# Output projections of a two-layer encoder: residual in token rows, norms per row tile inside the projection, activations as the stationary operand

## The reference, cut to what matters

```python
def rms_norm(x, g):
    y = xf * lax.rsqrt(jnp.mean(xf * xf, axis=-1, keepdims=True) + EPS)
    return (y * g.astype(jnp.float32)).astype(x.dtype)
...
    return jnp.concatenate([y_a, y_b], axis=-1) @ w_out      # layer 0: (1040, 2048) @ (2048, 1024)
...
    return (hh * jax.nn.silu(z)) @ w_out                     # layer 1: the same shapes
```

## Time and profile before

| | us |
|---|---|
| median of 3 runs (lowest, highest) | 3476.79 (3475.44, 3481.76) |
| span of the profiled execution | 3469.1 |
| what lies around that span, to the median | 7.7 |
| PE busy, share of the span | 2705.0, 78% |
| DVE busy | 1420.7, 41% |
| ACT busy | 912.4, 26% |
| POOL busy | 1079.5, 31% |
| mean granted clock of PE, share of full | 0.891 |

### The profile page before, as it was taken

How to read it: one execution, slowest core, us unless ns; L and a number is a source line. 1 busy time by engine, 2 the same in 40 slices (tenths; PEclk the granted TensorE clock), 3 DMA queues, 4 the chain that set the end, 5 groups by cost and what they waited for, 6 DMA issues and landing times. The chain is left out here.

```text
span 3469.1 us, 48250 instructions
## 1 busy us (share of the span) xinstructions
PE 2705.0 (78%) x16298; PEld 2337.1 (67%) x16298; DVE 1420.7 (41%) x2296; ACT 912.4 (26%) x1495; POOL 1079.5 (31%) x1228
## 2 busy tenths in 40 slices
PE   3778999359888645579929999969999656665995
PEld 2667888258877534569818888849999544444894
DVE  2713334437766654231063453431101356666204
ACT  1211222373333333321121222230100144443201
POOL 0422333017776000344214444314444211111540
PEclk7899999679999877799969999989999888888997
DMA  5212222500110133452113244252333254421412
GB/s 126 74 62 63 79 85 73 56 25 20 37 37 19 33 69 52 138 175 61 60 62 115 99 140 143 78 201 86 128 129 97 77 209 165 165 99 46 135 40 98
DMA packets 281662, 316.88 MB, mean 91 GB/s; under 512 B 43348, under 2 KB 235790, under 8 KB 279894
## 3 DMA queue, kind: packets, MB, share of 16 engines
q1 hardware_dynamic: 212854, 192.57, 18.9%
q10 hardware_dynamic: 68704, 123.16, 10.3%
HBM read 203.60 MB, written 107.87 MB: 90 GB/s over the span
## 5 line engine op out<-in xcount | busy, mean ns | idle before, releaser
L291 POOL TENSOR_TENSOR w_hi<-w_raw,ones 128x512 fp32r<-128x512 f32 (+1 forms) x312 | 342.7, 1098 | 1416.3 <-PE r L304 859.4
L292 POOL TENSOR_TENSOR w_lo<-w_raw,w_hi 128x512 fp32r<-128x512 f32 (+1 forms) x312 | 414.4, 1328 | 24.4
L304 PE MATMUL r<-h_lo,w_hi 128*128 128x264 f32 (+1 forms) x1344 | 306.2, 336 | 49.8 <-POOL w_lo L292 49.8
L304 PE MATMUL r<-h_hi,w_hi 128*128 128x264 f32 (+1 forms) x1344 | 288.3, 323 | 0.0
L304 PE MATMUL r<-h_hi,w_lo 128*128 128x264 f32 (+1 forms) x1344 | 286.4, 321 | 0.0
L304 PEld LDWEIGHTS r<-h_lo,w_hi 128*128 128x128 f32 x1344 | 200.5, 190 | 76.9 <-POOL w_lo L292 50.5
L304 PEld LDWEIGHTS r<-h_hi,w_lo 128*128 128x128 f32 x1344 | 195.0, 189 | 20.6
L304 PEld LDWEIGHTS r<-h_hi,w_hi 128*128 128x128 f32 x1344 | 194.4, 189 | 19.4
L304 PE MATMUL r<-x_lo,w_hi 128*128 128x264 f32 (+1 forms) x768 | 165.1, 323 | 45.3 <-POOL w_lo L292 35.0
L304 PE MATMUL r<-xc_lo,w_hi 128*128 128x264 f32 (+2 forms) x864 | 186.3, 324 | 5.6 <-ACT fx L1995 5.6
L385 DVE RECIPROCAL rstd<-rstd 128x1040 f32<-128x1040 f32 x4 | 26.6, 6653 | 392.8 <-ACT rstd L363 392.8
(11 more groups left out here) (338 smaller groups left out, 5278.6 us busy)
## 6 DMA issues: line engine op xcount, KB each, us to landing
w_raw<-in_w_in_even SPq DMA_DIRECT2D x72, 256.0 KB, 3.2
w_raw<-in_w_in_odd SPq DMA_DIRECT2D x64, 256.0 KB, 3.3
w_raw<-in_w_ogate SPq DMA_DIRECT2D x64, 256.0 KB, 5.1
v_d<-vs ACTq DMA_DIRECT2D x8, 1152.0 KB, 5.8
v<-v_d SPq DMA_DIRECT2D x8, 1152.0 KB, 11.3
h_hi<-cat_d ACTq DMA_DIRECT2D x16, 520.0 KB, 4.6
resid<-res_d SPq DMA_DIRECT2D x2, 4160.0 KB, 12.4
xc_d<-sg ACTq DMA_DIRECT2D x8, 1040.0 KB, 4.5
```

The source lines that it names most:

```text
L291: do(self.nc.gpsimd.tensor_tensor(hi, raw, one, ALU.mult))
L292: self.nc.gpsimd.tensor_tensor(lo, raw, hi.bitcast(F32), ALU.subtract).then_inc(self.split.sem, 1)
L304: ins = self.nc.tensor.matmul(region[:, PO + off:PO + off + n], w[:, b, k, :], z[:, off:off + n], start=(first and k == 0 and w is self.hi ...
```

## The change

The residual is kept token row by token row, as x comes in. `enter` becomes one stage: a tile of 116 rows is loaded, normed, transposed and split, and nothing is stored. `load_given` is issued by SP behind the row loads. `project_rows` takes the place of `project`, of three `norm_block` calls and of `leave`. In it the activations are stationary (116 or 128 tokens by 128 of K) and the weights move, 512 output features at a time, so that a row tile lies in PSUM in token rows. K goes in two halves of 8 tiles: after the first half ACT copies the sums out and stores them (`part`), after the second DVE adds them (`early`). The weights of a half stay in SBUF. The first three row tiles go through a half K tile by K tile together, the others one by one. ACT makes `w_hi`, POOL `w_lo`. DVE and ACT norm each row tile when its sum is there; for layer 0 PE transposes the normed tile (`turn_rows`, 8 transposes), ACT copies it to `h_hi` (`split_h`) and DVE makes `h_lo` (`lower`). Two rows of parameters less are loaded at the start.

```diff
-                    hi = sh.sb("h_hi", [P, KC, L], F32R)
-
-                    y = hi[:, :, :].bitcast(F32)
-                    project(nc, a["w_out_even"], d["cat"], c, y)
-                    h = [hi, sh.sb("h_lo", [P, KC, L], F32R)]
-                    with stage(nc) as s:
-                        res = s.sb("res", [P, KC, L])
-                        norm_block(nc, c, y, lambda k: c["col"]("norm_post", k), dst=res, resid=d["res"],
-                                   save=d["res"])
-                        norm_block(nc, c, res, lambda k: c["col"]("norm_pre", KC + k), split=h)
+                    h = [sh.sb(n, [P, KC, L], F32R) for n in ("h_hi", "h_lo")]
+                    project_rows(nc, a, d, c, a["w_out_even"], d["cat"], 0, ROWS, h=h)
                     conv_values_z(nc, a, c, d, h, gates)
                 raw = sg.sb("li", [40, L]), sg.sb("fx", [40, L])
                 odd_gates(nc, a, c, d, gates, raw)
                 gate_rows(nc, a, c, d, raw, cols)
             mlstm(nc, a, c, d, cols)
-        with stage(nc) as s:
-            y = s.sb("y", [P, KC, L])
-            project(nc, a["w_out_odd"], d["hh"], c, y[:, :, :])
-            res = s.sb("res", [P, KC, L])
-            norm_block(nc, c, y, lambda k: c["col"]("norm_post", KC + k), dst=res, resid=d["res"])
-            leave(nc, c, res, out)
+        project_rows(nc, a, d, c, a["w_out_odd"], d["hh"], 1, LAST_ROWS, out=out)
...
+ROWS = [(i * 116, min(116, L - i * 116)) for i in range(9)]
+LAST_ROWS = [(META + i * P, P) for i in range((L - META) // P)]
...
+            @block.sync
+            def _(sp):
+                for t, (off, m) in enumerate(ROWS):
+                    if t >= NB:
+                        sp.wait_ge(scaled, t - NB + 1)
+                    load_rows(sp, a, xt[:, t % NB, :], off, m, loaded[t % NB])
+                    if t == 0:
+                        sp.dma_start(gain[:, :], a["norm_pre"][0:D].unsqueeze(0).broadcast_to([P, D])
+                                     ).then_inc(gain_loaded, 16)
+                load_given(sp, a, given)
+
...
+def project_rows(nc, a, d, c, w_out, cat, layer, tiles, out=None, h=None):
+
+    HK, SL, HQ = KC, 3, KC // 2
+    NTL = len(tiles)
+    groups = [tiles[g:g + SL] for g in range(0, NTL, SL)]
+    NG = len(groups)
+    W = max(sum(m for _, m in g) for g in groups)
+    more = h is not None
+    NORMS = 2 if more else 1
...
+                    if at >= 2:
+                        sp.wait_ge(wl_done, 2 * (at - 1))
+                    sp.dma_start(wr[:, at % 2, :], wv[at]).then_inc(wl[at % 2], 16)
+
+                load_w(0)
+                load_x(0, 0, 0)
+                load_w(1)
+                load_x(0, 0, 1)
+                for at in range(2, HK):
+                    load_w(at)
+                for g in range(1, NG):
+                    for q in range(2):
+                        load_x(0, g, q)
+                load_w(HK)
+                load_w(HK + 1)
+                for j in range(NORMS):
+                    name, at = (("norm_post", layer), ("norm_pre", layer + 1))[j]
+                    sp.dma_start(gain[:, j, :], a[name][at * D:(at + 1) * D].unsqueeze(0).broadcast_to([P, D])
+                                 ).then_inc(gain_loaded, 16)
+                for g in range(2):
+                    for q in range(2):
+                        load_x(1, g, q)
+                for at in range(HK + 2, 2 * HK):
+                    load_w(at)
+                for g in range(2, NG):
+                    for q in range(2):
+                        load_x(1, g, q)
+
+                def fetch(t):
+                    off, m = tiles[t]
+                    b = t % 2
+                    sp.wait_ge(part_stored[b], 16 * (t // 2 + 1))
+                    if t >= 2:
+                        sp.wait_ge(added, 2 * t - 2)
+                        if more:
+                            sp.wait_ge(squared, 2 * t - 2)
+                            sp.wait_ge(scaled, t - 1)
+                        sp.wait_ge(stored[b], 16 * (t // 2))
+                    sp.dma_start(early[0:m, b, :], d["part"][t, 0:m, :]).then_inc(tile_loaded[b], 16)
+                    if more:
+                        load_rows(sp, a, resid[:, b, :], off, m, tile_loaded[b])
+                    else:
+                        sp.dma_start(resid[0:m, b, :], d["res"][off:off + m, :]).then_inc(tile_loaded[b], 16)
+                fetch(0)
+                fetch(1)
+                for t, (off, m) in enumerate(tiles):
+                    sp.wait_ge(made, t + 1)
+                    dst = d["res"][off:off + m, :] if more else out[off - META:off - META + m, :]
+                    sp.dma_start(dst, resid[0:m, t % 2, :]).then_inc(stored[t % 2], 16)
+                    if t + 2 < NTL:
+                        fetch(t + 2)
...
+                for at in range(2 * HK):
+                    gp.wait_ge(wh_done, at + 1)
+                    for n in range(2):
+                        cols = slice(n * 512, n * 512 + 512)
+                        nc.gpsimd.tensor_tensor(w[1][:, at % HK, cols], wr[:, at % 2, cols],
+                                                w[0][:, at % HK, cols].bitcast(F32), ALU.subtract).then_inc(wl_done, 1)
+
...
+                def products(hf, t, k):
+                    off, m = tiles[t]
+                    for p, q in ((1, 0), (0, 0), (0, 1)):
+                        for n in range(2):
+                            ins = nc.tensor.matmul(slot[(hf * NTL + t) % SL][0:m, n * 512:(n + 1) * 512], x[p][:, k, off:off + m],
+                                                   w[q][:, k, n * 512:(n + 1) * 512],
+                                                   start=(k == 0 and p == 1), stop=(k == HK - 1 and q == 1))
+                    return ins
+
+                def free_slot(hf, t):
+                    before = hf * NTL + t - SL
+                    if 0 <= before < NTL:
+                        pe.wait_ge(part_copied, 2 * before + 2)
+                    elif before >= NTL:
+                        pe.wait_ge(added, 2 * (before - NTL) + 2)
+
...
+                after = {3: (0,), 4: (1, 2), 5: (3,), 6: (4,), 7: (5, 6), 8: (7, 8)} if more else {}
+                for hf in range(2):
+                    for k in range(HK):
+                        pe.wait_ge(xl_done, hf * NG * HK + k + 1)
+                        pe.wait_ge(wl_done, 2 * (hf * HK + k + 1))
+                        for t in range(SL):
+                            if k == 0:
+                                free_slot(hf, t)
+                            ins = products(hf, t, k)
+                            if k == HK - 1:
+                                ins.then_inc(summed, 1)
+                    for t in range(SL, NTL):
+                        pe.wait_ge(xl_done, (hf * NG + t // SL + 1) * HK)
+                        free_slot(hf, t)
+                        for k in range(HK):
+                            ins = products(hf, t, k)
+                            if hf == 0 and t == NTL - 1 and k < HK - 1:
+                                ins.then_inc(w_used, 1)
+                        ins.then_inc(summed, 1)
+                        if hf == 1:
+                            for u in after.get(t, ()):
+                                turn_rows(u)
 
...
+                def w_hi(hf, k):
+                    at = hf * HK + k
+                    act.wait_ge(wl[at % 2], 16 * (at // 2 + 1))
+                    if hf:
+                        if k < HK - 1:
+                            act.wait_ge(w_used, k + 1)
+                        else:
+                            act.wait_ge(summed, NTL)
+                    nc.scalar.activation(w[0][:, k, :], wr[:, at % 2, :], ACT.Copy).then_inc(wh_done, 1)
+
+                def x_hi(hf, g):
+                    off, n = group_cols(g)
+                    for k in range(HK):
+                        if k % HQ == 0:
+                            act.wait_ge(xl[k // HQ], 16 * (hf * NG + g + 1))
+                            if hf and k == 0:
+                                act.wait_ge(summed, min((g + 1) * SL, NTL))
+                        nc.scalar.activation(x[0][:, k, off:off + n], xr[:, k, 0:n], ACT.Copy).then_inc(xh_done, 1)
+                        if hf == 0 and g == 0:
+                            w_hi(0, k)
+
+                def part_copy(t):
+                    m = tiles[t][1]
+                    act.wait_ge(summed, t + 1)
+                    if t >= 2:
+                        act.wait_ge(part_stored[t % 2], 16 * (t // 2))
+                    for n in range(2):
+                        cols = slice(n * 512, n * 512 + 512)
+                        nc.scalar.activation(part[0:m, t % 2, cols], slot[t % SL][0:m, cols],
+                                             ACT.Copy).then_inc(part_copied, 1)
+                    act.wait_ge(part_copied, 2 * t + 2)
+                    act.dma_start(d["part"][t, 0:m, :], part[0:m, t % 2, :]).then_inc(part_stored[t % 2], 16)
+
```

(118 more changed lines are left out.)

335 lines of the change are left out of this document (131 added, 204 removed).

## The result

The changed kernel takes 3353.82 us, median of 4 runs (3350.53 to 3359.64), against 3476.39 us before: ratio 0.9645, 95% interval 0.9631 to 0.9659. That is 123 us faster. The forecast was 3310 with a range of 3285 to 3348, so the direction is right and the time lies 44 us above it, 6 us outside the range. The profiled execution has a span of 3351.5 us.

What follows compares the result with a forecast made beforehand. PE bounds the projections and nearly idles in the norms behind them. Gains of 57.8 us (layer 0), 65.7 (layer 1) and 43 (`enter`), 166.5 in all, take the span from 3469.1 to 3302.6; plus 7.7 gives 3310, range 3285 to 3348.

Steps and rivals of the forecast that it cites:

- Stores of `part` and `early` loads lie beside products: Layer 0's projection: these transfers were taken as covered by products; uncovered they would cost 2.7 to 5.1 us a row tile.
- My fallback: Layer 0's projection: if products did not cover stores and loads, they would cost 2.7 to 5.1 us for a row tile.
- A: Layer 0's projection: moment when DVE can add the first row tile's two halves, forecast 145.2 us into the stage.
- DVE's chain: Layer 0 after the first sum: adds, norms, residual and `lower` for one row tile, forecast 10.3 us on DVE.
- The PSUM wait: End of a projection's first group: row tile 3 waits for a PSUM slot ACT must copy out, forecast 2.3 us.
- the 1 us charged between the halves: Projections: 1 us between the halves of K, where ACT remakes `w_hi` as PE frees each K tile.
- The matmul pace: Projections: 0.231 us per 512-column matmul, giving 199.6 us of products in layer 0 and 177.4 in layer 1.
- The rule of the Trainium skill: Matmul cost N/2.4 + 2.5 ns, 216 ns for 512 columns; 1632 matmuls would take 352 us, not the 377 forecast.
- The supply of weights: Rival, both projections: weight loading and splitting bind at 5.25 us a K tile, 35 us more, 3345 us; chance 0.14.
- The norm chain: Rival, layer 0: DVE binds at 12.5 us a row tile instead of 10.3, 21 us more, 3331 us; chance 0.10.
- the slower case: Projections: PE's clock stays at its lower level, gain used up at 44% of matmuls, all giving 3687 us; chance 0.03.
- the supply rival: Both projections: making the weights ready binds at 5.25 us a K tile, 35 us more, 3345 us; chance 0.14.

## Why the prediction was right and where it was wrong

**The step that failed** is the sentence "Stores of `part` and `early` loads lie beside products". I priced a transfer of a row tile at 2.7 to 5.1 us from transfers of 128 rows and saw it covered. In 116 rows it goes over 4 engines. A row tile has three of them, 16.2 us together, against 9.6 of DVE and 12 of PE. Six row tiles lose 6.3 to 7.6 us of DVE each before their adds (1662.01 to 1743.34), the seventh 0.3, 40.7 us in the sum that the waits give, and with tiles that divide by 16 the stage is 38.4 us shorter. My rows of the trace of before have no transfer of 116 rows, so nothing in them showed the price. The error was to move bytes from one shape to another at the same rate. My fallback, 2.7 to 5.1 us for a row tile, was wrong for the same reason, and also because it counted one transfer where three share the queue.

**Layer 0 otherwise.** With row tiles of 128 and 112 the stage takes 244.8 us for 240.8 forecast. From A on it is 95.2 for 95.6. PE's last sum closes it, at A + 82.1 for 82.6, and that this is so near is luck in part. DVE's chain is 0.7 us shorter per row tile than added (9.6 for 10.3). PE waits 2.87 us before the transposes of row tile 2 (2.8 forecast) and 1.53 before those of row tile 6 (4.2), but behind the first wait five pairs of matmuls run at the lower clock (granted 0.50 from 1658.6 to 1662.8) and take 2.1 us more, which the addition did not have:

```profile
1657.09 1.73 PE L555 MATMUL turn<-ident,y 112*128 112x112 f32 x8 [2.87 <-DVE h_lo L703]
```

Up to A it is 149.3 for 145.2. The PSUM wait was 4.57 for 2.3, the 2.2 us of lower clock behind it were not in the sum, the first matmul came at 10.6 for 9.6 (10.3 in the changed kernel), and the 1 us charged between the halves did not come. The matmul pace was right: eight pairs in 3.71 us (1559.63 to 1563.34) are 0.232 each, for 0.231. The rule of the Trainium skill (TensorE: Matmul & The Clock Gate, back-to-back issue gap), which that section gives for an isolated matmul, would have made the products of both layers 25 us shorter; the trace does not agree.

**Layer 1**, 205.1 for 200.8: the first matmul at 10.4 for 9.6, the wait 4.1 for 2.3, the lower clock behind it 2.5 (six pairs from 3195.79 to 3201.05). That is 5.1, where 4.3 are missing.

**enter**, 64.3 for 62, is two errors that nearly cancel, again luck. SP's row loads last until 39.3 and not 31.9, since each goes over 4 engines (30.0 with tiles that divide by 16). The 22 given loads took 24.3 us and not 28, and the next stage's first load came 0.7 behind them.

**The rivals.** The supply of weights did not bind: behind the first matmul PE has no wait for `w_lo` in either projection. The norm chain did not bind at 12.5 us: once the transfers are cured DVE has a period of 9.6 while it catches up with PE's 12, and at the last row tile it waits 2.56 us for PE's sum. PE's clock fell to 0.82 on average from A on in the changed kernel (0.92 with tiles that divide by 16): this is the mechanism of the slower case, in its small form, and the waits for transfers come first. No rival had the transfers in it. That the time, 3353.8, lies near the supply rival's 3345 is a coincidence.

## What to carry to other kernels

When a change alters the number of rows of a tile, price its transfers anew: look at the DMA line, and if it stands flat at a low share (0.25 at 116 rows, 0.12 at 118) while engines wait for "issue", look for the largest divisor of the row count up to 16. Choose row tiles that are multiples of 16, or cut the remainder off as a transfer of its own, before adding buffers. A wait in a dense run of matmuls costs more than itself: behind the one of 4.57 us the lower clock took another 2.2, behind that of 2.87 another 2.1. And work moved to a second queue is not free: beside the row loads of 116 rows it made the kernel 14.6 us slower.

## What the runs showed that I had not expected

A store of a row tile and the wait behind it take 2.7 us in 128 rows (layer 1), 8.3 in 116 and 5.75 in 119, with the tail of another reload before the last; a chain of three transfers per row tile has a period of 16.2 us at 116 rows and 30.0 at 118. Cutting 4 rows off a transfer of 116 and issuing it twice made the kernel 39 us faster. And an issue on SP of a transfer with many small pieces is longer, up to 4.6 us for 2.5 to 3.6, while other loads are under way.
